# Order of the first mixer's work around the substitution: decay rows, gate and Fourier tiles, GpSimd's scaling, zero fills, and the slots of two weight chunks

## What is computed

```python
p = h @ w_in                                   # u | q k v | z | rates
q, k, v = silu(conv(p[qkv])); q, k = l2norm(q), l2norm(k)
gc = cumsum(g)                                 # log decays in chunks
decay = exp(gc[:, None] - gc[None, :])         # lower triangle
a_mat = strict((k * beta) @ k.T * decay)
t_inv = inverse(eye + a_mat)                   # unit lower triangular
attn = lower(q @ k.T * decay)
u_val, w_key = t_inv @ (v * beta), t_inv @ (k * beta * exp(gc))
# scan over chunks, forward and backward, gives o
y_f = fourier(u) @ w_f                         # per group of channels
y_d = rmsnorm(o) * silu(z)
y = concat(y_f, y_d) @ w_out
```

## Time and profile before

| | us |
|---|---|
| median of 3 runs (1635.09 to 1635.15) | 1635.12 |
| the profiled execution | 1641.44 |
| its span, first to last instruction | 1639.6 |
| TensorE busy | 1342.9 |
| VectorE busy | 590.8 |
| ScalarE busy | 431.4 |
| GpSimd busy | 206.4 |

### The profile page before, as it was taken

One profiled execution on the slowest core, in us unless ns is written; L12 is line 12 of the kernel. 1 busy time (PEld: TensorE's weight loads), 2 busy tenths in 40 slices (PEclk: granted clock), 3 DMA queues, 4 the chain that ended last, 5 costly groups with the idle time before them and its releaser, 6 DMA issues.

```text
span 1639.6 us, 21764 instructions
## 1 busy us (share of the span) xinstructions
PE 1342.9 (82%) x9484; PEld 881.5 (54%) x9484; DVE 590.8 (36%) x1148; ACT 431.4 (26%) x643; POOL 206.4 (13%) x113
## 2 busy tenths in 40 slices
PE   7999899999999997676667758999977766675678
PEld 3787698999999942122212215999722212221226
DVE  4787656886277311011011104685201101100116
ACT  3554255444453210000000002583200000000005
POOL 0216224786410000000000000000000000000000
PEclk9999899999999898788787779999888878877889
DMA  9307453544647899999999999459799999999992
GB/s 400 144 1 274 185 225 124 191 153 151 228 173 285 328 418 426 428 427 427 427 428 427 427 424 392 150 210 378 287 426 427 428 428 426 427 427 426 427 410 102
DMA packets 52625, 528.44 MB, mean 322 GB/s; under 512 B 4784, under 2 KB 4912, under 8 KB 20144
## 3 DMA queue, kind: packets, MB, share of 16 engines
q1 hardware_dynamic: 51952, 525.22, 78.2%
q10 hardware_dynamic: 576, 1.79, 0.3%
HBM read 525.94 MB, written 1.05 MB: 321 GB/s over the span
## 4 chain that ended last, share of the span: by engine, by line
PE 53%; DMA 37%; DVE 4%; SPq 3%; ACT 1%; issue 1%; POOL 0%; DVEq 0%
PE bank L669 25%; PE bank L1275 9%; DMA ring<-in_w_up 8%; DMA ring<-in_w_down 7%; DMA work<-in_w_gate 7%; DMA ring<-in_w_gate 6%; DMA work<-in_w_up 4%; DMA work<-in_w_down 4%; PE bank L1295 3%; PE bank L1357 3%; SPq L563 2%; PE bank L889 2%; PE bank L1425 2%; DMA ring<-in_dense 2%; PE bank L662 2%; PE bank L741 1%
## 5 line engine op out<-in xcount | busy, mean ns | idle before, releaser
L1275 PE MATMUL bank<-ring,work 128*32 128x512 f32 x1232 | 320.8, 737 | 140.3 <-DMA ring<-in_w_up 71.9
L669 PE MATMUL bank<-work_rounded,ring_rounded 128*128 128x256 f32 (+1 forms) x2000 | 305.9, 288 | 2.2 <-DVE work_rounded L2066 1.2
L669 PEld LDWEIGHTS bank<-work_rounded,ring_rounded 128*128 128x128 f32 x2000 | 268.4, 190 | 9.6 <-issue 3.0
L669 PE MATMUL bank<-xn_rounded,ring_rounded 128*128 128x256 f32 (+1 forms) x1472 | 248.5, 285 | 1.2 <-DVE xn_rounded L2100 1.2
L1275 PEld LDWEIGHTS bank<-ring,work 128*32 128x32 f32 x1232 | 69.8, 131 | 313.3 <-issue 118.1
L2676 DVE TENSOR_TENSOR work<-work,bank 128x512 f32<-128x512 f32 x16 | 11.0, 687 | 547.4 <-PE bank L1275 547.4
L669 PEld LDWEIGHTS bank<-xn_rounded,ring_rounded 128*128 128x128 f32 x1472 | 202.6, 188 | 5.4 <-issue 2.7
L1275 PE MATMUL bank<-work 128*32 128x512 f32 x496 | 158.1, 679 | 33.9 <-DMA work<-in_w_gate 19.1
L1964 POOL TENSOR_TENSOR ring_rounded<-ring,ring_rounded 128x2048 fp32r<-128x2048 f32 (+1 forms) x35 | 148.8, 4269 | 163.2 <-ACT ring_rounded L1498 163.2
L2034 POOL TENSOR_TENSOR work<-work_rounded,work 128x128 f32<-128x128 f32 x32 | 12.1, 399 | 1068.0 <-PE bank L1332 728.4
L1498 ACT ACTIVATE ring_rounded<-ring 128x2048 fp32r<-128x2048 f32 (+1 forms) x76 | 133.0, 1795 | 49.5 <-PE bank L669 30.3
(11 more groups left out here) (338 smaller groups left out, 1718.2 us busy)
## 6 DMA issues: line engine op xcount, KB each, us to landing
ring<-in_dense SPq DMA_DIRECT2D x47, 2048.0 KB, 8.7
ring<-in_w_up SPq DMA_DIRECT2D x38, 2048.0 KB, 30.2
ring<-in_w_gate SPq DMA_DIRECT2D x36, 2048.0 KB, 29.8
ring<-in_w_down SPq DMA_DIRECT2D x34, 2048.0 KB, 29.2
work<-in_w_gate SPq DMA_DIRECT2D x16, 2048.0 KB, 23.6
work<-in_w_down SPq DMA_DIRECT2D x16, 2048.0 KB, 32.2
spare<-in_w_gate SPq DMA_DIRECT2D x8, 2048.0 KB, 28.9
work<-in_w_up SPq DMA_DIRECT2D x8, 2048.0 KB, 32.5
```

The source lines that it names most:

```text
L669: last = mm(out, rv(high_store[r][:, at:at + P]), rv(x[part][k]), start=opens and k == 0 and j == 0, stop=closes and k == n_k - 1 and j == 2)
L1275: ins = mm(out[slots(y), :], xg[:, k, slots(y)], expert_columns(w, at, 512), start=k == 0, stop=k == KT - 1)
```

## The change

- TensorE: `decay_rows(3)` and `beta_rows(2)` come ahead of the first gate tile. The first gate half is cut in its two tiles (`latent_tile`), with `decay_rows(4)` and `(5)` between them. The second gate half comes after all decay, key and beta products. The transposes of the values (`vtok`) come ahead of the Fourier halves. The first two chunks of `ada1` stand between these two halves, and the other two ahead of `dft_b`. The banks of rows 5 and 7 are 3 and 0 in place of 2 and 3.
- VectorE: differences and key matrices stand in another order, the two low halves apart among them, and `begc` comes after the substitution. The block transposes wait for the second gate half as well, whose weights lie where `blocks` does.
- GpSimd: the queries' scaling, one zero fill and the values' scaling, in this order. The two other zero fills go to ScalarE, as copies of a zero column (`tmat_zero`).
- ScalarE: the copies follow TensorE's new order, and the copy of `ada_rows(1)` comes ahead of the gate's activation.
- Loads: the slots of `ada1` are 1, 2, 1, 2 and of `ada2` 0, 1, 2, 0. `kd` lies in slot 1. The load of `w_out`'s second chunk no longer waits for `ds_mm` 6, that of `w_up`'s first chunk does.

```diff
-USES = [("ada0", 4), ("kv", 4), ("q", 2), ("v", 4), ("z", 2), ("u", 2), ("dft_w", 2), ("vtok", 4), ("ktok", 4), ("dft_b", 4),
+USES = [("ada0", 4), ("kv", 4), ("q", 2), ("v", 4), ("z", 2), ("vtok", 4), ("u", 2), ("dft_w", 2), ("ktok", 4), ("dft_b", 4),
...
-    for c, last in enumerate((4, 6, 10, 12, 14)):
+    for c, last in enumerate((4, 6, 10, 12, 18)):
...
-    held_until = {(first["w_out"], 3): ("vn_mm", 1), (first["w_out"] + 1, 0): ("ds_mm", 6),
+    held_until = {(first["w_out"], 3): ("vn_mm", 1), (first["w_up"], 1): ("ds_mm", 6),
...
-                r = (c + (1 if name == "ada1" else 2)) % (LOAD_SLOTS - 1)
+                r = ((1, 2, 1, 2) if name == "ada1" else (0, 1, 2, 0))[c]
...
-    kd = ring[0][:, 0:3072].rearrange("p (e h t) -> p e h t", e=6, h=HEADS)
+    kd = ring[1][:, 0:3072].rearrange("p (e h t) -> p e h t", e=6, h=HEADS)
...
+        def latent_tile(stage, c, b, i):
+
+            use, chunk, n = USE[stage] + b, FIRST["w_in"] + c, SEQ
+            if i == 0:
+                released(pe, use - BANKS)
+            for k in range(KT):
+                split_arrived(chunk, k)
+                last = split_product(bank[use % BANKS][:, n * i:n * i + n], chunk, 2 * b + i, x_lat, k)
+            if i:
+                assert signal(last, "dense_full") == use + 1
...
-        row_bank = (6, 0, 7, 1, 6, 2, 7, 3)
+        row_bank = (6, 0, 7, 1, 6, 3, 7, 0)
...
         decay_rows(2)
         beta_rows(0)
-        latent_half("z", 3, 0)
         released(pe, USE["v"] + 3)
         decay_rows(3)
         beta_rows(2)
+        latent_tile("z", 3, 0, 0)
         pe.wait_ge(S["at_ready"], 1)
         decay_rows(4)
-        latent_half("z", 3, 1)
-        released(pe, USE["z"])
         decay_rows(5)
+        latent_tile("z", 3, 0, 1)
         pe.wait_ge(S["at_ready"], 3)
         decay_rows(6)
         beta_rows(4)
-        released(pe, USE["z"] + 1)
+        pe.wait_ge(S["g_diff"], 2)
         decay_rows(7)
         pe.wait_ge(S["at_ready"], 4)
         key_products(2, 4)
         key_products(3, 5)
         beta_rows(6)
+        pe.wait_ge(S["qd_exp"], 2)
+        latent_half("z", 3, 1)
+        pe.wait_ge(S["qd_exp"], 4)
+        token_major("vtok", vc)
         latent_half("u", 4, 0)
+        ada_rows(1, (0, 1))
         latent_half("u", 4, 1)
         arrived(pe, FIRST["fourier"])
-        pe.wait_ge(S["qd_exp"], 4)
         for x, name in enumerate(("cos_c", "nsin_c")):
             dense(USE["dft_w"] + x, [(0, 512, [(fo(name), fo("w_f"))])])
 
...
         query_products(2, 4)
         query_products(3, 5)
 
-        token_major("vtok", vc)
         token_major("ktok", kc)
-        ada_rows(1, (0, 1))
+        ada_rows(1, (2, 3))
         for x in range(2):
             for u in range(NH):
                 dense(USE["dft_b"] + 2 * x + u, [
                     (P * g, P * g + P, [(uT[:, g, P * u:P * u + P], fo_w[:, x, P * g:P * g + P])]) for g in range(4)])
 
-        ada_rows(1, (2, 3))
...
-            if e in (3, 5):
-                to_sbuf("z", e // 4, wk("zs", 512, 512 * (e // 4)))
+            if e == 5:
+                to_sbuf("z", 0, wk("zs", 512))
             if e >= 4:
                 act.wait_ge(S["g_diff"], e + 1)
-                signal(act.activation(qd[:, e - 4], paired(by_head(bank[(6, 2, 7, 3)[e - 4]])), ACT.Exp), "qd_exp")
+                signal(act.activation(qd[:, e - 4], paired(by_head(bank[(6, 3, 7, 0)[e - 4]])), ACT.Exp), "qd_exp")
             act.wait_ge(S["g_masked"], e + 1)
             if e >= 4:
                 att = attnT[:, e - 4]
                 signal(act.activation(att, paired(amat[:, d, u]) if d == 0 else att, ACT.Exp), "att_exp")
             signal(act.activation(amat[:, d, u], amat[:, d, u], ACT.Exp, scale=1.0 - 2.0 * d), "decay")
 
+        to_sbuf("z", 1, wk("zs", 512, 512))
+        for u in range(4):
+            to_sbuf("vtok", u, wk("vtok", 512, 512 * u))
         for b in range(2):
             to_sbuf("u", b, wk("oT", 512, 512 * b))
         for x in range(2):
             to_sbuf("dft_w", x, fo_w[:, x])
-        for stage, tile in (("vtok", "vtok"), ("ktok", "ktok")):
-            for u in range(4):
-                to_sbuf(stage, u, wk(tile, 512, 512 * u))
+        for u in range(4):
+            to_sbuf("ktok", u, wk("ktok", 512, 512 * u))
+        nothing = c_cols[:, 0, 0:1]
+        signal(act.activation(ring[LOAD_SLOTS][:], nothing.to_broadcast([P, CHUNK]), ACT.Copy), "tmat_zero")
...
+        act.wait_ge(S["dense_full"], USE["dft_b"] + 4)
+        signal(act.activation(wk("oT"), nothing.to_broadcast([P, 1024]), ACT.Copy), "tmat_zero")
+        ada_rows(1)
         functions(SILU)
         signal(act.activation(wk("zs"), wk("zs"), ACT.Silu), "silu_ready")
         functions(LN_EXP)
...
-        pool.wait_ge(S["dense_full"], USE["z"] + 2)
-        pool.memset(solved, 0.0).then_inc(S["tt_zero"], 1)
         for e in range(4):
             u = token_of(2 + e // 2, e % 2)
             pool.wait_ge(S["qd_exp"], e + 1)
             pool.tensor_tensor(qd[:, e], qd[:, e], paired(qc[:, :, columns_of(u)]), ALU.mult).then_inc(S["qd_ready"], 1)
-        pool.wait_ge(S["dense_full"], USE["u"] + 2)
-        pool.memset(ring[LOAD_SLOTS][:], 0.0).then_inc(S["tt_zero"], 1)
+        pool.wait_ge(S["dense_full"], USE["z"] + 2)
+        pool.memset(solved, 0.0).then_inc(S["tt_zero"], 1)
         for u in range(4):
             released(pool, USE["vtok"] + u)
-        for d in range(2):
-            for u in range(4):
+        for u in range(4):
+            for d in range(2):
                 pool.tensor_tensor(xv[d][:, u], vtok[:, u], bc(beta[:, u, 4 * d:4 * d + 4], shape), ALU.mult)\
                     .then_inc(S["scaled_v"], 1)
-        pool.wait_ge(S["dense_full"], USE["dft_b"] + 4)
-        pool.memset(wk("oT"), 0.0).then_inc(S["tt_zero"], 1)
         pool.wait_ge(S["solved"], 2)
-        pool.wait_ge(S["tt_zero"], 3)
+        pool.wait_ge(S["tmat_zero"], 2)
+        pool.wait_ge(S["scaled_v"], 8)
...
         key_matrix(0)
+        difference(3)
         key_matrix(1)
-        weights_low(FIRST["w_in"] + 4)
-        for e in range(3, 8):
-            difference(e)
-            key_matrix(e - 1)
-        key_matrix(7)
-        dve.wait_ge(S["gc_exp"], 1)
-        for d in range(2):
-            last = v.scalar_tensor_tensor(begc[:, d], beta[:, :, 4 * d:4 * d + 4], -1.0, egcol[:, d], ALU.mult, ALU.mult)
-        signal(last, "gate_cols")
-
+        key_matrix(2)
+        weights_low(FIRST["w_in"] + 4, (0,))
+        difference(4)
+        difference(5)
+        key_matrix(3)
+        weights_low(FIRST["w_in"] + 4, (1,))
+        difference(6)
+        key_matrix(4)
+        difference(7)
+        for e in range(5, 8):
+            key_matrix(e)
...
         dve.wait_ge(S["at_ready"], 8)
+        dve.wait_ge(S["dense_full"], USE["z"] + 2)
...
-        dve.wait_ge(S["tt_zero"], 2)
+        dve.wait_ge(S["gc_exp"], 1)
+        for d in range(2):
+            last = v.scalar_tensor_tensor(begc[:, d], beta[:, :, 4 * d:4 * d + 4], -1.0, egcol[:, d], ALU.mult, ALU.mult)
+        signal(last, "gate_cols")
+        dve.wait_ge(S["tmat_zero"], 2)
...
-        dve.wait_ge(S["tt_zero"], 3)
```

More of the change, by code:

```diff
@@ L253 @@
     "gate_cols", "gc_exp", "kk_mm", "g_rows", "b_rows", "g_diff", "g_masked", "decay", "qd_exp", "att_exp",
-    "at_ready", "qk_mm", "att_ready", "solved", "tt_zero", "diag_act", "diag_pool", "scaled_v", "qd_ready",
+    "at_ready", "qk_mm", "att_ready", "solved", "tt_zero", "tmat_zero", "diag_act", "diag_pool", "scaled_v", "qd_ready",
     "kd_ready", "ks_mm", "rest_ready",
@@ L1650, in _ @@
         functions(LN_EXP)
-        ada_rows(1)
         for b in range(2):
@@ L1659, in _ @@
             signal(act.activation(p5[high_block, :, 2 * s:2 * s + 2], x, ACT.Copy), "join_act")
-        act.wait_ge(S["tt_zero"], 2)
-        act.wait_ge(S["tt_zero"], 3)
+        act.wait_ge(S["tmat_zero"], 2)
         act.wait_ge(S["solved"], 1)
@@ L2306, in _ @@
         dve.wait_ge(S["gate_cols"], 2)
-        row_bank, key_bank = (6, 0, 7, 1, 6, 2, 7, 3), (4, 5, 4, 5)
+        row_bank, key_bank = (6, 0, 7, 1, 6, 3, 7, 0), (4, 5, 4, 5)
         def difference(e):
```

## The result

| | before | after |
|---|---|---|
| median, us (21 runs each) | 1635.33 | 1641.68 |
| lowest to highest | 1632.53 to 1642.45 | 1637.0 to 1649.31 |
| the profiled execution | 1641.44 | 1647.23 |
| its span | 1639.6 | 1645.4 |

The ratio is 1.0041, 95% interval 1.003 to 1.0052: 6.35 us slower. The forecast was 1638.2. So the direction of the sum was right and the time lies inside the range, but the loss came out twice as large as its +3.1. It also lies beyond the 0.2% up to which I would have called it no change (0.50), on the slower side (0.43).

What follows compares the result with a forecast made beforehand. The joins' start was taken to be set by when TensorE's queries' products end and how long VectorE's substitution takes behind them. 8.8 + 0.2 - 5.9 = +3.1 us on the 1635.12 median gave 1638.2 us, range 1634.5 to 1642.5.

Steps and rivals of the forecast that it cites:

- the sum: Whole kernel: 8.8 us lost at the queries' products, 0.2 added for VectorE, 5.9 gained in the substitution, +3.1 us.
- GpSimd's scaling, 5.9 us: VectorE's substitution: eight steps slowed by GpSimd's scalings run short once these are moved off it, 5.9 us gained.
- The gate, 131.5: TensorE's gate tiles: decay rows ahead of them make the gate end between 130.6 and 132.5, taken as 131.5.
- rival 2: Gate on TensorE: ends late, at 132.5, so the sum is +4.1 and the time 1639.2 us; chance 0.20.
- The second chunk 13.9 us behind the gate: Load between the Fourier halves: lands 13.9 us behind the gate and holds TensorE until 145.4.
- The first chunk: First load between the Fourier halves: lands only about 9 us behind the gate; TensorE waits about 1 us.
- The clock, 1.00 between 140 and 156: TensorE around the chunks and Fourier halves: granted clock expected to stay 1.00 between 140 and 156.
- Rival 1: Waits before the second Fourier half: clock falls, 2 to 6 us more on the path, 1643 us; chance 0.18.
- The sum of the path: TensorE up to the queries' products: they end at 156.4 in place of 147.56, 8.8 us later.
- The 0.2 us for VectorE: VectorE's four products behind the queries' products: 0.2 us added, since the first no longer runs ahead.
- From the joins on: Rest of the kernel: priced at 0, 0.5 us either way; a shift here goes through to the end.
- Rivals 3 and 4: 3: second chunk doesn't hold TensorE, sum -1.5 us, chance 0.14; 4: scaling doesn't slow the substitution, 1644 us, chance 0.03.

Runs made afterwards that it cites:

- 4: Kernel before with GpSimd's eight value scalings moved behind the copies that follow the substitution; 1633.15 us, ratio 0.9969.
- 6: Changed kernel with VectorE's second low half of the Fourier weights moved behind the last key matrix; 1639.27 us, ratio 1.0024.
- 1: Changed kernel with the first two chunks of `ada1` back behind the queries' products and the keys' transposes; 1635.63 us, ratio 0.9997.
- 5: Changed kernel with two chunks' loads issued ahead of the Fourier constants' load and the queries' products ahead of both Fourier halves; 1627.26 us, ratio 0.995.
- 8: Changed kernel with two chunks' loads issued early, queries' products ahead of the Fourier halves, second low half behind the last key matrix; 1623.25 us, ratio 0.9917.
- 7: Changed kernel with the first two `ada1` chunks back behind the queries' products and the old slots of `ada1` and `kd`; 1631.64 us, ratio 0.997.

## Why the prediction was right, and where it fell short

**GpSimd's scaling, 5.9 us: right.** 29.4 to 23.5 us, to a tenth, and 4 shows it by that edit alone.

**The gate, 131.5: it was 132.35 (130.78 + 1.57).** This was rival 2, at the late end of the range, by the mechanism given: the mask waited for VectorE's low half. The Trainium skill's rule ("SBUF — State Buffer", section "Who interferes with whom") would have given 132.5, and the traces agree: VectorE's low half waited for a mask and the next mask for it in after, and with the low half moved away, in 6, the gate ends 1.85 us earlier. I had halved the difference for lack of a row; the whole of it came. 0.85 us.

**The second chunk 13.9 us behind the gate: it landed 15.7 behind.** This term of the sum was mis-sized. I read the landing from DMA shares of the earlier trace rows, as the end of the busy windows. The trace of before has the landing itself; the issues of SyncE between 124 and 126 say:

```profile
L523 SPq DMA_DIRECT2D ring<-in_dense x3: 327/430/432, 124.3 to 125.1; - x3
...
DMA to landing us min/median/max: 4.6/10.0/14.4
```

The third load is issued at 125.1 and lands 14.4 later, at 139.5, which is 15.3 behind the gate, not 13.9. So 1.4 us of the 1.8 is my reading. In after, it is issued at 131.7 and lands 14.8 later, and that is the other 0.4. The first chunk was misread in the same way: it landed 10.9 us behind the gate (141.64 - 130.78), not about 9, and TensorE's first wait was 3.46 us and not about 1. In before, the share was 0.06 from 138 on, 1.5 us ahead of the landing: it doesn't show when the last bytes are there.

**The clock, 1.00 between 140 and 156: it was 0.50 from 142 to 152.** Rival 1 (0.18) came on top of the forecast. The chunk cost 3.64 us for 1.80, the Fourier half 6.93 for 5.65: 3.1 us.

**The sum of the path.** The queries' products ended at 160.60 + 1.57 = 162.2 where I had 156.4. The difference, 5.8, is 0.85 + 1.8 + 3.1. So the end was 14.6 us later than before, not 8.8. Less 5.9, the joins start 8.7 us later (188.01 + 1.57 = 189.58 against 180.90). The 0.2 us for VectorE didn't come: its four products end 1.9 us behind the queries' (162.50 and 160.60), as before.

**From the joins on.** I had priced this at nothing. TensorE is idle for 6.30 us before them, and the clock is 0.50 in all windows from 188 to 202. Before, it was 0.50 in fewer: from 182 to 188, after the idle 3.12 us, and again from 200 to 202, though TensorE had had no idle time since 180.90 (the last products ahead of this fall, at 198.8, were of 64x64). The product behind the scan, which was at 228.36 before, stands at 237.95, 11.2 later in the stage, so 2.5 us more were lost here:

```profile
237.95 1.55 PE L1098 MATMUL bank<-work,consts 128*128 128x512 f32 x3 [0.69 <-ACT work L1714]
```

**From the stage to the median, where luck comes in.** I had written that a shift here goes through to the end. In the pair of profiles it doesn't: the distance is 11.2 us at the end of the stage and 7.4 at the end of the program, counted from the same product (5.8 between the two executions, and 1.57), and the medians differ by 6.35. With all 11.2 the time would have been some 1646.5, outside my range, which ended at 1642.5; that 1641.68 lies inside it is in part luck, since I hadn't foreseen that the distance shrinks on the way. The profiles show the place where it happens. The window from 1140 to 1160, in the second block, of before and of after:

```profile
1140.00:1160.00 20.00, 20.00 (x98) 18.98 (x98) 7.17 (x31) 5.31 (x10) 0.00 (x0) 0.61 0.74 281
```

```profile
1140.00:1160.00 20.00, 20.00 (x107) 17.86 (x105) 4.80 (x12) 2.18 (x4) 0.00 (x0) 0.91 0.85 328
```

The granted clock was 0.61 in the one and 0.91 in the other, and there the distance between them shrinks from 10.5 + 1.57 to 5.6 + 1.57 us. In experiments 1 and 4 the clock there is 0.63 and 0.57, in the six others 0.83 or more. It doesn't go with any edit that I can name, and what sets it stays open. Stage and median part in other runs too: counted to the product behind the scan, 5 is 11.3 and 8 is 10.7 us shorter than before, and their medians are 7.4 and 11.4 lower. The executions of before and of after spread over 10 and 12 us, those of 7 over 15.6, so one profile can't carry a difference of 5.

**Rivals 3 and 4** are excluded: TensorE waited, and the steps got short.

## What to carry to other kernels

An instruction that waits for a load holds everything behind it on its engine, so work that starts the longest chain goes ahead of it: the same edits that lost 6.35 us give 7.4 when the queries' products stand ahead of the chunks and the two loads ahead of the one that waits (5), and 11.4 with the second low half behind the last key matrix as well (8). When two engines end close together, as here substitution and TensorE's list, shortening one is worth only the distance to the other (5.9 us of work, 2.3 of time). Read a landing from the issue's own time to landing and not from the share of busy DMA engines.

## What was not expected of the hardware

- Two waits of 3.46 and 1.78 us with 16 products between them cost 10 us at half clock; four and three products of 512 columns inside them kept it at 1.00. In 6, with waits of 3.37 and 1.62, the clock was 0.50 for some 3 us only, and the second chunk's products ran in 1.92 us. The waits of the two are the same to within 0.2 us; what decides stays open.
- GpSimd and VectorE waited for each other in both directions where both worked from SBUF in long instructions: a mask of 1.27 us took 3.3, and a low half of 2.28 took 3.21. Yet GpSimd's eight scalings took 8.21 us beside the substitution's short steps and 8.03 alone: here only VectorE paid, 1.04 for 0.32.
